# A four-layer network in float32r pairs: moving operand read in blocks of 16 from alternating halves, weight rooms paired by address

## What is computed

```
first_block:   layer 0:  x += s5_mixer(rms_norm(x))          # state space, then gelu @ w_glu
               layer 1:  x += diff_attention(rms_norm(x), shared_kv(x))
               each:     x += conv_ffn(rms_norm(x));  x += sigmoid(rms_norm(x) @ w_gate) * (p @ w_proj)
second block:  layer 2:  x += even_mixer(rms_norm(x))        # top-k attention and pooling
               layer 3:  x += odd_mixer(rms_norm(x))         # stick-breaking attention
               each:     x += swiglu(rms_norm(x), w1, w3, w2)

conv_ffn: up = h @ w_up (1024 -> 2 x 2816); three-tap causal convolution; (gelu(g) * val) @ w_down
swiglu:   (silu(h @ w1) * (h @ w3)) @ w2    (1024 -> 2816 -> 1024)
```

## Time and profile before

| | |
|---|---|
| Median of three runs | 1310.41 us (1309.94 to 1310.79) |
| The profiled execution, its own time | 1310.93 us |
| Its span in the profile | 1309.2 us |
| PE, busy share of the span | 98% |
| POOL, busy share | 77% |
| ACT, DVE, busy shares | 52%, 49% |
| Granted TensorE clock, mean | 0.998 |
| DMA queue of the weights, share of 16 engines | 45.5% |

### The profile page before, as it was taken

One profiled execution on the slowest core, in us unless ns is written; L12 is line 12 of the kernel. 1 busy time (PEld: TensorE's weight loads), 2 busy tenths in 40 slices (PEclk: granted clock), 3 DMA queues, 4 the chain that ended last, 5 costly groups with the idle time before them and its releaser, 6 DMA issues.

```text
span 1309.2 us, 27666 instructions
## 1 busy us (share of the span) xinstructions
PE 1278.9 (98%) x10976; PEld 1228.8 (94%) x10976; DVE 641.3 (49%) x1163; ACT 681.7 (52%) x944; POOL 1003.9 (77%) x793
## 2 busy tenths in 40 slices
PE   6999999999999999999999999999999999999999
PEld 5889999999989889999999878999999999999998
DVE  8995575555555748555555575211113454411112
ACT  7725544444676756434446565544346666644442
POOL 1226998889677659988887794988987766989985
PEclk9999999999999999999999999999999999999999
DMA  6304675555534334555554532555554433555530
GB/s 272 130 34 163 183 260 182 176 187 192 189 135 166 125 130 170 193 179 177 189 193 142 203 134 82 199 181 190 192 185 153 165 116 130 193 193 190 185 138 33
DMA packets 33879, 217.07 MB, mean 166 GB/s; under 512 B 3683, under 2 KB 7428, under 8 KB 8196
## 3 DMA queue, kind: packets, MB, share of 16 engines
q1 hardware_dynamic: 30096, 211.14, 45.5%
q10 hardware_dynamic: 3700, 4.75, 1.5%
HBM read 213.26 MB, written 2.62 MB: 165 GB/s over the span
## 4 chain that ended last, share of the span: by engine, by line
PE 83%; DVE 8%; ACT 5%; issue 2%; POOL 1%; DMA 0%; DVEq 0%; SPq 0%; ACTq 0%; POOLq 0%
PE up L1576 18%; PE up L1578 17%; PE up L1577 17%; PE acc L1576 7%; PE acc L1578 6%; PE acc L1577 6%; PE up L1711 2%; DVE opnd L980 2%; PE side L1803 2%; ACT w_hi L511 1%; PE acc L1769 1%; ACT opnd L649 1%; PE side L1584 1%; DVE mix L985 1%; PE up L1842 1%
## 5 line engine op out<-in xcount | busy, mean ns | idle before, releaser
L421 POOL TENSOR_TENSOR w_lo<-ring,w_hi 128x512 fp32r<-128x512 f32 x748 | 953.4, 1309 | 222.3 <-ACT w_hi L511 219.2
L1576 PE MATMUL up<-opnd,w_hi 128*128 128x256 f32 x2064 | 588.2, 285 | 4.1 <-DVE opnd L980 1.6
L1577 PE MATMUL up<-opnd,w_lo 128*128 128x256 f32 x2064 | 578.5, 280 | 0.0
L1578 PE MATMUL up<-opnd,w_hi 128*128 128x256 f32 x2064 | 578.1, 280 | 0.0
L511 ACT ACTIVATE w_hi<-ring 128x2048 fp32r<-128x2048 f32 x188 | 359.4, 1913 | 250.1 <-PE up L1578 191.2
L1576 PEld LDWEIGHTS up<-opnd,w_hi 128*128 128x128 f32 x2064 | 388.5, 188 | 16.6 <-issue 13.8
L1577 PEld LDWEIGHTS up<-opnd,w_lo 128*128 128x128 f32 x2064 | 390.2, 189 | 1.3 <-issue 1.0
L1578 PEld LDWEIGHTS up<-opnd,w_hi 128*128 128x128 f32 x2064 | 388.9, 188 | 0.0
L1576 PE MATMUL acc<-opnd,w_hi 128*128 128x256 f32 x784 | 221.7, 283 | 1.4 <-DVE x L1226 1.2
L1578 PE MATMUL acc<-opnd,w_hi 128*128 128x256 f32 x784 | 220.6, 281 | 0.0
L1577 PE MATMUL acc<-opnd,w_lo 128*128 128x256 f32 x784 | 219.7, 280 | 0.0
(11 more groups left out here) (296 smaller groups left out, 1424.4 us busy)
## 6 DMA issues: line engine op xcount, KB each, us to landing
ring<-in_stream SPq DMA_DIRECT2D x197, 1024.0 KB, 4.8
bias_rows<-mix ACTq DMA_DIRECT2D x1, 1536.0 KB
mix<-in_s_b SPq DMA_DIRECT2D x1, 1024.0 KB, 6.3
x<-in_x SPq DMA_DIRECT2D x1, 1024.0 KB, 8.3
mix<-in_s_c SPq DMA_DIRECT2D x1, 1024.0 KB, 12.3
mix<-bias_rows ACTq DMA_DIRECT2D x1, 1024.0 KB, 5.7
out_x<-x SPq DMA_DIRECT2D x8, 128.0 KB, 1.7
mix<-in_p ACTq DMA_DIRECT2D x2, 256.0 KB, 3.5
```

What stands on the lines that cost most here:

```text
L421: ins = nc.gpsimd.tensor_tensor(w_l[:, cols], ring[:, r, cols], w_h[:, cols].bitcast(f32), ALU.subtract)
L1576: MM(o, l_hi, r_hi, start=start, stop=False, skip_group_check=True)
L1577: MM(o, l_lo, r_hi, start=False, stop=False, skip_group_check=True)
L1578: return MM(o, l_hi, r_lo, start=False, stop=stop, skip_group_check=True)
```

## The change

Two things are changed together. The helper `three` hands the output and both moving operands through `blocked`, a view that turns 256 columns into 8 blocks of [2 halves, 16 columns]: columns 0 to 15, 128 to 143, 16 to 31, 144 to 159, and so on. Each column of the result stays in its place; only the order in which the columns are read and written differs. A half is 128 columns, 512 bytes; a block is 64 bytes. In a values slot the moving operand is the weight room, and it is read in that order too.

`HOMES` lists the rooms in another order, so that the high and the low room of the same number follow each other. The pads are the same in sum, and everything from x on keeps its address. From `opnd0` the rooms are now at 0 and 0 (room 0), 64 and 64 (room 1), 192 and 192 (room 2) bytes modulo 256; from `opnd1`, at 192, 0 and 128. No instruction is added, removed or moved.

```diff
-HOMES = [(0, 0, 0), (1, 1, 0), (1, 0, 16), (0, 1, 0), (1, 2, 0), (0, 2, 32)]
+HOMES = [(0, 0, 0), (1, 0, 0), (0, 1, 16), (1, 1, 0), (0, 2, 32), (1, 2, 0)]
 OPND_PADS = (16, 16)
+BLOCK = 16
...
+            def blocked(v):
+
+                return v.rearrange("p (t b c) -> p b t c", t=2, c=BLOCK)
+
             def three(o, l_hi, l_lo, r_hi, r_lo, start, stop):
 
+                o, r_hi, r_lo = blocked(o), blocked(r_hi), blocked(r_lo)
                 MM(o, l_hi, r_hi, start=start, stop=False, skip_group_check=True)
                 MM(o, l_lo, r_hi, start=False, stop=False, skip_group_check=True)
                 return MM(o, l_hi, r_lo, start=False, stop=stop, skip_group_check=True)
```

## The result

| | before | after |
|---|---|---|
| Median | 1310.6 us (1309.94 to 1311.57, 4 runs) | 1327.74 us (1327.25 to 1328.35, 4 runs) |
| Profiled execution, own time | 1310.93 us | 1328.35 us |
| Span in the profile | 1309.2 us | 1326.6 us |

The changed kernel is slower: the ratio is 1.0131, with a 95% interval of 1.0118 to 1.0144. I had forecast 1286 us, faster. The time lies within the range of 1268 to 1345, but on the other side, in the case that I had called "the runs cost".

A forecast was written before the change was run, and what follows sets the result against it. PE's matmuls in three lines bound the kernel. Freeing all slots would give 26.6 + 8.8 = 35.4 us; with one distance still clashing, a middle gain of 25 off 1310.9 gave 1286 us, range 1268 to 1345.

The forecast's parts named there:

- the runs cost: Rival, chance 0.16: 15 further runs add 6.3 ns a matmul; 1326 us on 113.3 ns, 1368 on 117.9, middle 1345.
- The bound: PE, busy 98% of 1309.2 us, mostly in three matmul lines; one nanosecond on each of 9216 matmuls is 9.2 us.
- The price is the distance between starts: Matmuls overlap, so their 280 to 285 ns duration is no price; start to start is 117.9 ns, 5.66 us a slot.
- The quick pace: Eleven slots at 5.44 us, 113.3 ns a matmul, taken as clash-free; each freed slot gains 0.22 us.
- The block order frees the slots: Moving operand and weight load both advance 64 bytes, so they no longer pass; 35.4 us gained if all slots are freed.
- The shape of the access: Sixteen runs instead of one in operand and output: bounded between nothing and 6.3 ns a matmul, taken as nothing.
- The sum: One distance keeps its clash; gains of 20.4 to about 31 us by which one, middle 25, giving 1286 us; chance 0.34.
- The output's pattern in PSUM costs nothing: Output written in 64-byte runs: of two skill sentences, the one on pairs of consecutive elements was followed, so no cost.
- POOL stays behind PE: POOL's low weight parts take 5.20 us a slot, under 5.44, leaving 0.2 to 0.4 us spare; nothing given back.
- all free: Rival, chance 0.20: one stall sets the two reads apart in every pair, all slots at 5.44 us; 1275 us.
- a standing clash: Rival, chance 0.20: reads at distance 0 meet in every block, 71 slots at 6.32 us; slower, 1337 us.
- no effect: Rival, chance 0.10: the 4.6 ns between paces come from something neither order nor address touches; 1310 us.

## Why the prediction was wrong, point by point

**The bound: right.** PE's three lines set the time, one nanosecond on each of 9216 matmuls is 9.2 us. It holds for the result, too: 2.4 ns would be 22 us; in the feed-forward stages, where PE never stands idle, 132 slots x 0.113 us = 14.9 us against 14.0 measured, and of the others' 60 x 0.113 = 6.8 us half, 3.4 us, arrived.

**The price is the distance between starts: right.** In the changed kernel three starts take 0.36 us, and each record still shows 0.28 us:

```profile
923.98 0.28 PE L1582 MATMUL up<-opnd,w_hi 128*128 128x256 f32 x1
...
924.34 0.28 PE L1582 MATMUL up<-opnd,w_hi 128*128 128x256 f32 x1
```

**The quick pace is the one without a clash between the moving read and the next load: right**, by the held load (113.7 ns, 276 ns a matmul), and its size as well: I took 0.22 us a slot, and 3.9 ns x 48 = 0.19 us is what a held load gave. Of the 60 slots in the other stages I kept two thirds; with the held load they gave some 4 us of 60 x 0.19 = 11.3, so little over a third was left. That term was too high, but no sign hung on it. That it is a matter of addresses equal modulo 256: not shown. The blocks with the old rooms (1328.15 us), with 32 bytes between (1328.73 us) and with the new ones (1327.74 us) are within 0.2 ns in pace, and both held reads show no distance either. Against it speak the rooms alone, where slots of one room and one operand take 5.66 and 5.45 us in turn. And I had said that below 5.44 us the weight load would have to be shorter; with the moving operand held and ordinary loads a slot took 5.36, so it was not the load that stood there.

**The block order frees the slots: right in that the clash no longer costs anything** (it adds 0.0 ns with 16 runs), **and not borne out in what I put it down to.** I had the two addresses go forward together; but then the rooms ought to matter, and they don't. A slower read that hides the clash would do the same.

**The shape of the access, "I take nothing": this is the step that failed.** The term was 6.3 ns a matmul, 58 us over 9216 of them if nothing were hidden, against a gain of 3.9 ns where the clash was; with it at nothing the sum came out at 25 us gained, and 17 were lost. The lower end of that term, nothing, came from the earlier trace rows, where four matmuls with two runs each start 117.5 ns apart, "no more than one run costs". The upper end, one cycle for each of 15 further runs, 6.3 ns, was what came: 120.0 ns is 113.3 and 6.7, or 6.3 on the 113.7 of the held load. That it fits so well is in part luck, since 32 and 64 runs do not cost a cycle each. The rows could not carry what I laid on them. By the line through 1, 8 and 16 runs one further run costs 0.42 ns, which is less than a timeline of 0.01 us over four matmuls can tell; and they were at the common pace, in which the clash stood, so that a longer read need not have shown at all: with 8 runs the clash already adds only about half. A bound from below has to be read where the term it bounds is not hidden under another, and over as many repeats as the term will have.

**The sum** for that was in the text as the lower branch of the rival "the runs cost": 6.3 ns on 113.3, 5.74 us a slot, 1326 us. 5.76 us and 1327.74 us came. The other branch, 6.3 ns on top of the common pace and 1368 us, does not happen: with 16 runs clash and runs do not add up. I took the middle of the two (1347, not the 1345 that I wrote) instead of asking which it would be. With a chance of 0.16 on it I let rows of two runs weigh more than that nothing in the program has more than two.

**The output's pattern in PSUM costs nothing: right** (1313.65 us with 32 runs written, 1313.81 with one). The Trainium skill, Advanced Engine Details and Errata, PSUM Cachelines, has a non-contiguous pattern slow matmuls significantly, and pairs as what counts. The runs agree with the second on the write; what did slow the matmuls was the pattern of the read from SBUF, which the section does not tell apart.

**POOL stays behind PE: right**, and with more to spare. POOL's timeline in the changed kernel, with the idle time before and its releaser:

```profile
920.42 5.05 POOL L422 TENSOR_TENSOR w_lo<-ring,w_hi 128x512 fp32r<-128x512 f32 x4 [0.70 <-ACT w_hi L512]
```

0.70 us, after 0.62 in a common slot of before. In the quick kernels the cover held as well: in a slot of 5.36 us POOL is busy 4.93.

**The signature that I had named** for "the runs cost", all slots alike and over 5.7 us, is what the stretches show. The three others fell: no slot was at 5.44 (all free), none over 5.95 (a standing clash; its term had the largest price and did not occur at any of the four distances), and the mixture is gone (no effect).

**What stays open**: what sets the pace in one run between 113.3 and 121 ns, since addresses bear on it but slots with the same ones differ; how the clash comes about; whether the price goes by the number of runs or by steps of 3.3 ns as they get shorter. None of the kernels with the reference's products beats the one before: to have the 27 us of the clash one would need a moving read in one run that does not meet the load, and neither layout tried gave it (1313.81 and 1317.97 us).

## What to carry to other kernels

Where PE sets the time, cut the moving operand's read into as few runs as can be, and take a price for it from measured patterns: here 3 ns a matmul for 8 runs, 6.3 for 16, 9 to 10 for 32, with no load in the way, while the pattern of the output in PSUM was free down to runs of 32 bytes. When an edit removes one cost by making something slower, measure both apart: hold one of two reads at one address and the clash between them shows by itself, without any instruction or wait changed. And where the profile has no row for a shape, give its upper bound a weight of its own, and do not take a nothing read from rows in which another cost stands.

## What the runs showed of the hardware that I had not expected

- Reading the moving operand in runs costs the matmul time: 113.7 ns with one, 116.7 with 8, 120.0 with 16, loads held; 123.3 and 127.1 with 32 and 64 beside ordinary loads. That is one cycle of 2.4 GHz a run up to 16, or some 3.3 ns for each halving of the runs from 128 bytes down; both fit.
- The load of the next weights and the moving read of a matmul cost PE time together: 117.6 ns against 113.7 with the load held at one address, 111.7 with the moving operand held.
- 113.3 ns is no floor. With the moving operand held every slot took 5.36 us, 111.7 ns a matmul.
- A start of the operands 32 bytes on costs 0.5% in one run (1317.97 us, ratio 1.0034 to 1.0068), and hardly anything in 16 runs (1328.73 against 1327.74 us).
